# Two sets of triangular inversions, woven apart or run step by step together, in a one-core kernel of three transformer layers

## What is computed

```python
lower = jnp.where(strict, beta[..., :, None] * kk * decay, 0.0)
rhs = jnp.concatenate([beta[..., None] * v, (beta * jnp.exp(gc))[..., None] * k], axis=-1)
sol = lax.linalg.triangular_solve(lower, rhs, left_side=True, lower=True, unit_diagonal=True)
...
def step(state, inp):
    u_c, w_c, q_c, a_c, k_c, ge = inp
    delta = u_c - jnp.einsum('bhcd,bhde->bhce', w_c, state)
    o = jnp.einsum('bhcd,bhde->bhce', q_c, state) + jnp.einsum('bhij,bhje->bhie', a_c, delta)
    state = ge[..., None, None] * state + jnp.einsum('bhcd,bhce->bhde', k_c, delta)
    return state, o
```

```python
a_qk = jnp.einsum('bhnid,bhnjd->bhnij', q * jnp.exp(bc - b_ref), k * jnp.exp(b_ref - bc))
o_intra = jnp.einsum('bhnij,bhnje->bhnie', jnp.where(incl, a_qk, 0.0), v)
...
o = jnp.einsum('bhcd,bhde->bhce', q_c, state) + oi_c
state = ge[..., :, None] * state + jnp.einsum('bhcd,bhce->bhde', k_c, v_c)
```

## Time and profile before

| | |
|---|---|
| Time, median of 3 runs | 1253.07 us (1252.16 to 1253.15) |
| The profiled execution's own time | 1253.0 us |
| Its span, first to last instruction | 1251.8 us |
| TensorE busy | 1243.3 us, 99% of the span |
| VectorE, ScalarE, GpSimd busy | 814.0, 691.2 and 140.8 us |
| Mean granted TensorE clock | 0.999 |

### The profile page before, as it was taken

One profiled execution on the slowest core, in us unless ns is written; L12 is line 12 of the kernel. 1 busy time (PEld: TensorE's weight loads), 2 busy tenths in 40 slices (PEclk: granted clock), 3 DMA queues, 4 the chain that ended last, 5 costly groups with the idle time before them and its releaser, 6 DMA issues.

```text
span 1251.8 us, 17456 instructions
## 1 busy us (share of the span) xinstructions
PE 1243.3 (99%) x7066; PEld 1032.8 (83%) x7066; DVE 814.0 (65%) x1114; ACT 691.2 (55%) x1046; POOL 140.8 (11%) x119
## 2 busy tenths in 40 slices
PE   9999999999999999999999999999999999999997
PEld 8888888888888888888888887888888888888886
DVE  5657755566788556655567888846875765755654
ACT  6665644443778645444447755546855363645543
POOL 1130000000221200000000322000320000211112
PEclk9999999999999999999999999999999999999999
DMA  8755466865454648555545534333456544565652
GB/s 296 229 158 185 147 223 202 267 187 164 152 164 157 216 155 253 190 181 178 181 148 188 184 121 150 119 103 102 135 202 235 173 147 133 170 214 171 204 169 85
DMA packets 127697, 220.18 MB, mean 176 GB/s; under 512 B 8336, under 2 KB 71184, under 8 KB 127616
## 3 DMA queue, kind: packets, MB, share of 16 engines
q1 hardware_dynamic: 123360, 205.95, 51.2%
q0 software_dynamic: 2672, 10.20, 2.4%
q10 hardware_dynamic: 1584, 2.92, 0.6%
HBM read 215.88 MB, written 3.15 MB: 175 GB/s over the span
## 4 chain that ended last, share of the span: by engine, by line
PE 96%; issue 1%; DMA 1%; ACT 1%; DVE 0%; POOL 0%; ACTq 0%; SPq 0%; POOLq 0%
PE ps L403 25%; PE ps L405 25%; PE ps L404 25%; PE ps L503 5%; PE ps L504 2%; PE ps L820 1%; PE ps L420 1%; PE ps L677 1%; PE ps L808 1%; PE ps L1058 1%; PE ps L1073 1%; DMA ar<-in_mem 0%; PE ps L779 0%; DMA raw<-in_w_gate_up 0%; PE ps L607 0%
## 5 line engine op out<-in xcount | busy, mean ns | idle before, releaser
L1615 DVE TENSOR_TENSOR spl<-raw,spl 128x1024 fp32r<-128x1024 f32 x387 | 477.4, 1258 | 102.8 <-ACT spl L1106 101.2
L1106 ACT CAST spl<-raw 128x1024 fp32r<-128x1024 f32 x387 | 400.1, 1050 | 181.7 <-PE ps L405 88.1
L403 PE MATMUL ps<-spl,xs 128*128 128x512 f32 x928 | 371.3, 400 | 0.0
L405 PE MATMUL ps<-spl,xs 128*128 128x512 f32 x928 | 362.2, 390 | 0.0
L404 PE MATMUL ps<-spl,xs 128*128 128x512 f32 x928 | 361.4, 389 | 0.0
L405 PEld LDWEIGHTS ps<-spl,xs 128*128 128x128 f32 x928 | 174.1, 188 | 37.4
L403 PEld LDWEIGHTS ps<-spl,xs 128*128 128x128 f32 x928 | 174.4, 188 | 35.8 <-issue 1.5
L404 PEld LDWEIGHTS ps<-spl,xs 128*128 128x128 f32 x928 | 174.5, 188 | 34.1 <-issue 0.5
L403 PE MATMUL ps<-spl,ys 128*128 128x512 f32 x496 | 198.5, 400 | 0.1
L405 PE MATMUL ps<-spl,ys 128*128 128x512 f32 x496 | 193.7, 391 | 0.0
L404 PE MATMUL ps<-spl,ys 128*128 128x512 f32 x496 | 193.2, 390 | 0.0
(11 more groups left out here) (329 smaller groups left out, 1146.5 us busy)
## 6 DMA issues: line engine op xcount, KB each, us to landing
raw<-in_w_in SPq DMA_DIRECT2D x112, 512.0 KB, 3.7
raw<-in_w_gate_up SPq DMA_DIRECT2D x176, 256.0 KB, 4.1
raw<-in_mlp_w SPq DMA_DIRECT2D x64, 512.0 KB, 4.4
raw<-in_w_down SPq DMA_DIRECT2D x44, 512.0 KB, 4.5
raw<-in_w_out SPq DMA_DIRECT2D x24, 512.0 KB, 4.1
raw<-in_xattn_wk SPq DMA_DIRECT2D x8, 512.0 KB, 4.0
raw<-in_xattn_wv SPq DMA_DIRECT2D x8, 512.0 KB, 4.4
raw<-in_w_branch_gdn SPq DMA_DIRECT2D x8, 512.0 KB, 3.2
```

The source lines that it names most:

```text
L403: self.do.matmul(bank, xh, hi, start=start, stop=False)
L405: m = self.do.matmul(bank, xl, hi, start=False, stop=stop)
L1106: self.do.copy(self.k.spl[:, u % NH, 0, :], self.k.raw[:, u % NR, :]).then_inc(*self.up("hi", (u,)))
L1615: self.do.tensor_tensor(lo, self.k.raw[:, u % NR, :], hi.bitcast(F32), ALU.subtract).then_inc(*self.up("lo", (u,)))
```

## The change

Only numbers in the table of the third layer change. The parts of the two `gdn_mid` flows from level 0 on now have the same step numbers, 37 to 50, so that each part of set 0 is followed at once by the same part of set 1. The two `gdn_scan` flows and `gla` get later or denser numbers: scans at 51 to 55 and 55 to 59, `gla` at every step from 50 to 63.

```diff
-         (gdn_mid(E, 0), (13, 17, 18, 19, 21, 22, 23, 24, 26, 28, 30, 32, 33, 35, 37, 38, 40, 41, 42, 43, 44)),
-         (gdn_mid(E, 1), (30, 32, 33, 34, 36, 37, 38, 39, 40, *range(41, 53))),
+         (gdn_mid(E, 0), (13, 17, 18, 19, 21, 22, 23, 37, 38, *range(39, 51))),
+         (gdn_mid(E, 1), (28, 31, 32, 33, 34, 35, 36, 37, 38, *range(39, 51))),
...
-         (gdn_scan(E, 0), (45, 46, 47, 48, 49)), (out_gdn(E, 0), (57, 58, 59)),
-         (gdn_scan(E, 1), (53, 55, 57, 58, 60)), (out_gdn(E, 1), (61, 62, 63)),
-         (gla(E), (46, 47, 48, 49, 50, 51, 53, 54, 55, 56, 57, 59, 61, 63)),
+         (gdn_scan(E, 0), (51, 52, 53, 54, 55)), (out_gdn(E, 0), (57, 58, 59)),
+         (gdn_scan(E, 1), (55, 56, 57, 58, 59)), (out_gdn(E, 1), (61, 62, 63)),
+         (gla(E), tuple(range(50, 64))),
...
-         (out_gla(E, 0), (62, 63, 65)), (part(og, 2), (66, 67)), (ya(), (65, 66)))
+         (out_gla(E, 0), (63, 64, 65)), (part(og, 2), (66, 67)), (ya(), (65, 66)))
```

## The result

The changed kernel takes 1261.95 us, the median of six runs (1261.3 to 1262.26), beside 1252.76 us for the kernel before (six runs, 1252.16 to 1253.15): a ratio of 1.0072, with a 95% interval from 1.0061 to 1.0082. It is slower by 9.2 us, where I forecast 3.7. The profiled execution took 1262.26 us, with a span of 1261.0 us and a mean granted clock of 0.997.

A forecast was written before the change was run, and what follows sets the result against it. The prediction took TensorE's work and waits to bound the kernel. From 1253.0 us it took 2.4 for joins and added 6.1 for waits in set 1's scan, giving 1256.7 us, range 1250.8 to 1260.0.

The forecast's parts named there:

- the part on the levels: Steps 38 to 50: each part needs results from one unit earlier; waits costed at nothing.
- level 0: Eight VectorE instructions at step 37 for products at step 38, the tightest place; if late, at most 0.3 us.
- the clock: Sign of a wrong prediction: clock granted at less than full in the waits; no price given.
- the scan's waits: Set 1's scan among GLA's exponentials: TensorE waits 1.6, 2.0 and 2.6 us, together 6.1 us.
- the joins: Groups of 64x64 products at 13 places instead of 21: eight joins gain 2.4 us, between 2.0 and 2.8.
- POOL's L2262: Needed by the cross part at step 60, now behind a power of `out_gdn`: costed at nothing, upper end 2.8 us.
- a product that waits in steps 38 to 50: Sign of a wrong prediction: any product waiting in these steps, where waits were costed at nothing.
- (1): Profile after: TensorE waits at L1412 (1.6 us), L1992 (2.0) and L1407 (2.6), nothing that size elsewhere in the layer.
- That the waits don't come: Rival: slack in ScalarE's queue removes all three scan waits, only joins count: 1250.6 us, chance 0.17.
- sum to 2 to 4.5 us: Rival: scan chain partly shorter, by quicker VectorE or slower TensorE: 1252.6 to 1255.1 us, chance 0.17.
- That more comes late behind: Rival: POOL's part (up to 2.8 us) and level 0 (0.3 us) come late: 1257 to 1260 us, chance 0.06.
- The dearer table load: Rival: ScalarE's load behind the full-width logarithm waits for its drain, chain 1.1 us later: 1257.8 us, chance 0.04.

The follow-up runs named there:

- e1: Kernel before, with only parts 1 to 7 of set 1's `gdn_mid` at the changed kernel's steps (28, 31 to 36): 1253.02 us, ratio 1.0000.
- e2: Changed kernel with the square and power parts of set 1's key convolution one step earlier (28 and 29): 1259.9 us, ratio 1.0054.
- e5: Changed kernel with the edits of e2 and e4 together: 1257.66 us, ratio 1.0037.
- e8: e5 with the last two scan parts of set 1 one step later (55, 56, 57, 59, 60): 1257.67 us, ratio 1.0033.
- e11: e10 with `out_gdn` of set 0 at 58 to 60 and not 60 to 62: 1256.38 us, ratio 1.0028.
- e6: Changed kernel with the edits of e2, e3 and e4 together: 1256.07 us, ratio 1.0023.
- e7: e6 with the last two scan parts of set 1 one step later (55, 56, 57, 59, 60): 1255.07 us, ratio 1.0015.
- e10: e6 with `gla` without step 55, ending at 64, set 1's scan at 55, 56, 57, 59, 61, outputs one step later or more: 1257.11 us, ratio 1.0035.
- e4: Changed kernel with level 0 of set 0 at step 35 instead of 37: 1260.5 us, ratio 1.0059.
- e3: Changed kernel with the first two gates (tanh parts) at steps 47 to 49 instead of 55 to 57: 1261.56 us, ratio 1.0063.

## Why the prediction was right in its direction and wrong in its size

**The step that failed** is the part on the levels, "I cost the waits here at nothing", and with it that the text never walks the seven early parts of set 1, steps 28 and 31 to 36, at all. What it put at nothing ahead of the scans cost 6.0 us: 2.9 at L796, 1.7 at level 0 and 1.4 of clock. The change doesn't only put work where it is new; it also takes 64x64 groups of 0.8 to 1.3 us away from between the units at steps 26 to 35, and they were the cover of the chain power, L1917, L1905, split, L1931 ahead of L796. e1 (moved, with cover: nothing) and e2 (moved, no cover, power earlier: no wait) bound the cause from two sides; the case of cover gone and parts unmoved is not shown. I named the cover of what the change adds; here it was the cover of unchanged work that went.

**The account.** Wait at L796 2.9, the clock 1.4, level 0 1.7, the scan's waits 5.8, the joins -2.35 us: 9.45, where the layer's distance grew by 9.43 us. The agreement is no test: the first three are differences of the same distances, and the joins are what e5 has left over. What can be checked apart is that the five waits stand in the table, and the price of a join.

- *The joins*: forecast 2.4 us for eight, 0.30 each; 2.35 us are left over in e5, 0.29 each. In the profile after, two parts b in one run, 128 records, take from 801.21 to 803.89, less 0.46, 2.22 us, and twice 1.29 us apart, a saving of 0.36 us; why the mean lies below that I only estimated, from groups that 128-wide products follow:

```profile
801.21 0.39 PE L405 MATMUL ps<-spl,xs 128*128 128x512 f32 x1
801.53 2.10 PE L820 MATMUL ps<-ar 64*64 64x64 f32 x128
...
803.89 0.39 PE L404 MATMUL ps<-spl,xs 128*128 128x512 f32 x1
```

- *Level 0*: named as the tightest place, and mis-sized, at most 0.3 us against 1.7. Two waits are named for L1951 (0.61 and 0.43 us), one for each set's four masks. I had counted the queue as one mask behind, but the eight masks alone take longer than a unit of 2.74 us, and start only after the split (timeline of DVE after, TensorE's last large product ahead of them at 790.11):

```profile
789.42 3.12 DVE L1951 TENSOR_TENSOR ar<-ar,con 64x256 f32<-64x256 f32 x8
```

- *The scan*: right. Counted from 869.97, the delta part was forecast to start at 14.3, solve 1 at 20.8 and the read at 27.05; they started at 14.34, 20.74 and 26.91. The three waits, forecast as 1.6, 2.0 and 2.6, were 1.6, 1.8 and 2.4 us, for the releasers named. The differences are of TensorE a little later and VectorE and ScalarE a little earlier than walked, 0.1 us each.
- *POOL's L2262*, costed at nothing: right in the changed kernel, where L988 doesn't wait (POOL in answer to the earlier trace rows), though the power ahead of it comes late, as I said:

```profile
896.62 2.57 POOL L2218 TENSOR_TENSOR sml<-sml 128x8 f32<-128x8 f32 x1 [34.94 <-DVE sml L1682]
899.17 2.39 POOL L2262 TENSOR_TENSOR ar<-ar 128x1024 f32<-128x1024 f32 x1
```

  TensorE's own waits of 5.8 us hide it, as far as the other runs show: in e8 and e11, where less of them is left and the power stands ahead of L2262 as well, L988 waits 1.8 and 2.1 us.
- *The clock*: the prediction named it as what would make it wrong, gave it no price and left it out of the range. It was 1.4 us. Of the signs by which the prediction would be wrong, this one came, and so did a product that waits in steps 38 to 50 (L820, at 38). The dearest wait, at L796, lies at step 33 and was under none of these, though it goes against (1), nothing of that size elsewhere in the layer.

**The rivals.** That the waits don't come, or sum to 2 to 4.5 us, fell with the 5.8 us. That more comes late behind was right in level 0 and wrong in its place for POOL, and its price reached only to 1260 us. The dearer table load fell: the second load starts 0.02 us after the logarithm has ended (879.32 + 1.06 = 880.38, then 880.40) and the tanh 0.01 us after the load. From the logarithm's start to that of the tanh are 2.37 us, of which the switch is 1.31. By the 2.66 us of the Trainium skill, page "ScalarE: Activation LUTs", section "What ACT_TABLE_LOAD costs", it would be 3.72 by estimate; this trace doesn't agree with the drain that the page counts, neither behind a copy nor behind a full-width activation.

**Where the gain went.** With the two places ahead of the scans mended (e5), what remains is a trade: 2.35 us of joins against a scan of set 1 that starts later and shares ScalarE, VectorE and POOL with GLA. In each of e6, e7, e8, e10 and e11 a wait that was removed came back in part at another product of the same stretch, and none of them is faster than before. Whether some other layout would be is open.

## What to carry to other kernels

When parts are gathered in one place, walk the place that they leave as well: small groups between large ones are cover for whatever chain runs beside them, unchanged work too. A chain over three engines could be forecast to 0.2 us here by walking each queue in its new order with the paces of the trace. Such a walk holds only for the products that it covers: what e7, e8, e10 and e11 missed lay for the most part at products that I had not walked. It is worth doing for every stretch that the change touches, not only for the one that looks tight. And a wait of 1.5 to 2.5 us on TensorE should get the price of a slow stretch behind it as an upper end, 1.5 us here.

## What the runs showed of the hardware that I had not expected

- **A slow stretch behind some waits, not behind others.** In it the granted clock is 0.50, and it cost 1.4 to 1.65 us (B of e2 and e4 less that of e5: 1.47 and 1.63). It came at L796 after waits of 1.5 and 1.0 us in the changed kernel and in e3 and not in e4, whose waits there were the same; at the third wait of the scan in e2 and e4 and not in e5, with waits within 0.1 us of theirs; behind L988 in e8 and e11, after waits of 1.8 and 2.1 us. The traces of e5, e6, e7 and e10 show none in this layer. Each kernel has one trace, so whether the kernel or the single execution decides isn't known; the spread of e5 speaks for the execution, the same place in the changed kernel and e3 for the kernel. What picks the place stays open.
- **VectorE and POOL hold each other up.** The same split L1615 takes 1.22 us alone and 2.32 us beside POOL's L2234, and two L1931 take 1.28 and 3.20 us. In e2, where VectorE was ahead, it is the other way round: the split takes 1.22 us and L2234 is recorded with 4.71 us where it has 1.72 us after:

```profile
762.84 4.71 POOL L2234 TENSOR_TENSOR ar<-ar,con 128x512 f32<-128x512 f32 x1 [7.91 <-ACT ar L1370]
```

  In the changed kernel L2234 ran from 762.93 for 1.72 us, to 764.65, and the split began at 763.40; had it stood still until 764.65, it would end at 765.87 with its 1.22 us, and it ended at 765.72, within 0.15 us. The Trainium skill, page "SBUF — State Buffer", section "SBUF: two separate sides", says that an operation of VectorE with two inputs in SBUF and one of GpSimd take a shared pair of ports as an exclusive lock, each for its whole instruction; the trace agrees.
